# Two alternating places for the first expert matrices, and the next pair's ahead of the down matrices

## What is computed

```python
def grouped_moe(x, w_router, w1, w3, w2):        # w1, w3: [16, 1024, 512], w2: [16, 512, 1024]
    aff = jax.nn.sigmoid(t @ w_router)
    ...                                          # best group of 4 experts, best 2 of it, weights sum to 1
    for e in range(N_EXPERTS):
        h = jax.nn.silu(t @ w1[e]) * (t @ w3[e])
        y = y + gates[:, e:e + 1] * (h @ w2[e])
```

## Time and profile before

| | |
|---|---|
| median of the runs | 1598.01 us |
| profiled execution | 1597.01 us |
| its span | 1595.2 us |
| TensorE busy | 1527.3 us, 96% |
| DMA moved | 425.27 MB, mean 267 GB/s |
| TensorE waits for DMA of w1 and w3, layer 0 | 5.1 us |
| the same, layer 1 | 3.9 us |

### The profile page before, as it was taken

One profiled execution on the slowest core, in us unless ns is written; L12 is line 12 of the kernel. 1 busy time (PEld: TensorE's weight loads), 2 busy tenths in 40 slices (PEclk: granted clock), 3 DMA queues, 4 the chain that ended last, 5 costly groups with the idle time before them and its releaser, 6 DMA issues.

```text
span 1595.2 us, 20497 instructions
## 1 busy us (share of the span) xinstructions
PE 1527.3 (96%) x8300; PEld 1038.2 (65%) x8300; DVE 904.8 (57%) x1338; ACT 646.5 (41%) x1028; POOL 40.9 (3%) x67
## 2 busy tenths in 40 slices
PE   8999999997999999999989999999999999999998
PEld 7775334333887743433357775799887777678997
DVE  4886111115887731111189864687787974757555
ACT  5352111112643421111067764544456766444443
POOL 0100000000000000000040000000002000000000
PEclk9999999999999999999999999999999999999999
DMA  9967999999564599999954545567864354447541
GB/s 313 328 229 314 421 427 428 428 423 288 176 205 154 213 397 422 428 426 428 411 186 159 190 153 195 178 237 287 300 255 170 129 203 170 173 159 279 196 159 27
DMA packets 116140, 425.27 MB, mean 267 GB/s; under 512 B 5117, under 2 KB 7641, under 8 KB 102601
## 3 DMA queue, kind: packets, MB, share of 16 engines
q1 hardware_dynamic: 112384, 416.76, 68.6%
q0 software_dynamic: 2304, 6.95, 1.5%
q10 hardware_dynamic: 1352, 0.18, 0.1%
HBM read 421.78 MB, written 1.05 MB: 265 GB/s over the span
## 4 chain that ended last, share of the span: by engine, by line
PE 69%; DMA 14%; DVE 8%; ACT 4%; DVEq 3%; issue 2%; SPq 0%; ACTq 0%
PE bank L656 42%; DMA ring<-in_moe_w 9%; PE bank L1533 9%; PE bank L1551 4%; DMA arena<-in_moe_w 3%; PE bank L2832 2%; DVE ring_r L3086 1%; PE bank L1563 1%; PE bank L1503 1%; PE bank L858 1%; DMA ring<-in_w_ff 1%; PE bank L2834 1%; PE bank L2735 1%; ACT in_whi L2916 1%; PE bank L2755 1%
## 5 line engine op out<-in xcount | busy, mean ns | idle before, releaser
L1533 PE MATMUL bank<-ring,arena 128*64 128x512 f32 x896 | 226.0, 595 | 9.0 <-DMA ring<-in_moe_w 9.0
L656 PE MATMUL bank<-ring_r,x_hi 128*128 128x512 f32 x528 | 207.7, 393 | 0.0
L607 DVE TENSOR_TENSOR parts_dit<-ring,parts_dit 128x2048 fp32r<-128x2048 f32 x66 | 151.3, 2292 | 74.7 <-ACT parts_dit L604 74.7
L604 ACT CAST parts_dit<-ring 128x2048 fp32r<-128x2048 f32 x66 | 125.1, 1899 | 95.4 <-PE bank L656 83.0
L656 PE MATMUL bank<-parts_dit,f_hi 128*128 128x512 f32 x512 | 160.4, 394 | 0.3 <-DVE parts_dit L607 0.3
L656 PE MATMUL bank<-x_hi,parts_dit 128*128 128x256 f32 x896 | 160.6, 281 | 0.0
L1533 PEld LDWEIGHTS bank<-ring,arena 128*64 128x64 f32 x896 | 74.2, 137 | 117.4 <-issue 117.1
L1856 DVE TENSOR_TENSOR arena<-arena,bank 128x512 f32<-128x512 f32 x16 | 17.2, 1075 | 225.5 <-PE bank L1533 225.5
L656 PEld LDWEIGHTS bank<-x_hi,parts_dit 128*128 128x128 f32 x896 | 137.8, 188 | 0.5
L656 PE MATMUL bank<-in_whi,x_hi 128*128 128x512 f32 x304 | 124.5, 410 | 1.3 <-DVE x_lo L2534 0.8
L656 PE MATMUL bank<-x_lo,parts_dit 128*128 128x256 f32 x448 | 125.3, 280 | 0.0
(11 more groups left out here) (383 smaller groups left out, 2663.8 us busy)
## 6 DMA issues: line engine op xcount, KB each, us to landing
ring<-in_moe_w SPq DMA_DIRECT2D x52, 2048.0 KB, 17.8
arena<-in_moe_w SPq DMA_DIRECT2D x36, 2048.0 KB, 18.5
ring<-in_w_ff SPq DMA_DIRECT2D x32, 2048.0 KB, 9.0
ring<-in_w_ada SPq DMA_DIRECT2D x24, 2048.0 KB, 8.9
ring<-in_w_in SPq DMA_DIRECT2D x20, 2048.0 KB, 9.2
ring<-in_mlstm_w_in SPq DMA_DIRECT2D x8, 2048.0 KB, 15.6
ring<-in_gla_w_in SPq DMA_DIRECT2D x5, 2048.0 KB, 13.2
ring<-in_moe_w SPq DMA_DIRECT2D x8, 1024.0 KB, 17.6
```

The costliest lines, as they stand in the source:

```text
L604: return nc.scalar.copy(part_view(where, 0, h, form), half_of(ring[:, SLOT_OF[n], :], form, h))
L607: return nc.vector.tensor_tensor(part_view(where, 1, h, form), half_of(ring[:, SLOT_OF[n], :], form, h), part_view(where, 0, h, form).bitc ...
L656: last = pe.matmul(out, a[ka], b[kb], start=(first and i == 0), stop=(final and i == 2))
L1533: last = pe.matmul(bank[halves[h], :], s_x[p // 2 % 2][:, c, at:at + CAP], w[h][:, c, :], start=(c == 0), stop=(c == DC - 1))
```

## The change

There are now two places for w1 of odd pairs, `SECOND` and `SECOND + 1` (`DOUBLE = 2`), so that both roles 0 and 1 alternate. There are eight places in all. The arena grows by 16 KB per partition (21536 to 25632 elements). `SECOND` lies in the new part, where no mixer writes. The fourth extra place lies over the row vectors and 4 KB ahead of them.

- `second_of_odd`: the first w1 matrix of pair 1 is issued right behind the last matrix of the mixer's output projection, before the stage of the experts.
- The second w1 matrix of pair 1 goes last of the first burst, when the output projection is done and 3 (layer 0) or 8 (layer 1) uses of row vectors are counted.
- From pair 1 on SyncE's order is w3 of p, w1 of p + 1, w2 of p. The last pair has w3 and w2 alone.
- The row vectors 3 and 8, and with them those behind them, wait on GpSimd until the w1 matrices of the layer's last pair are used.
- The mask `dil` is no longer in the table; it is loaded into `SECOND` behind the second input matrix of the second block, when the experts are done with it.

The core of the diff:

```diff
-        rows = sb("rows", [P, ROW_SLOTS, D])
-        kst = sb("kst", [P, CONST_N])
+        kst = sb("kst", [P, KEPT_N])
...
+        ROWS_AT, SECOND_AT = 72.125, 84.125
+        rows = area(ROWS_AT, ROW_SLOTS * D, (ROW_SLOTS, D))
+        dil = area(SECOND_AT, TT * 2 * T, (TT, 2 * T))
...
-        more_slots = area(36, (ROLES + 1 - SLOTS) * SLOT, (ROLES + 1 - SLOTS, SLOT))
+        more_slots = [area(at, SLOT) for at in (36, 52, SECOND_AT, ROWS_AT - 4)]
...
-            return SECOND if k == 0 and p % 2 else k
+            return SECOND + k if k < DOUBLE and p % 2 else k
...
-            return NP * l + (p - 1 if k == 0 else p)
+            return NP * l + (p - 1 if k < DOUBLE else p)
...
+        ROWS_LEFT = (3, 8)
+
+        def second_of_odd(sp, l):
+
+            if l:
+                sp.wait_ge(e_free[0], NP * l)
+            sp.dma_start(e_slot(SECOND, FE), A["moe_w1"][l, 2].rearrange("(p c) n -> p c n", p=P)).then_inc(
+                e_landed[SECOND], 16)
...
+            def first_of_pair(sp, l, k, p):
+                sp.wait_ge(e_free[k], last_use(k, l, p))
+                sp.dma_start(e_slot(place_of(k, p), FE), A["moe_w1"][l, 2 * p + k].rearrange("(p c) n -> p c n", p=P)).then_inc(
+                    e_landed[place_of(k, p)], 16)
+
             for p in range(NP):
-                for k in by_release if p == 0 else range(ROLES):
+                order = range(ROLES) if p < 2 else range(DOUBLE, ROLES)
+                for k in by_release if p == 0 else order:
                     if p == 1 and k == 0:
+                        continue
+                    elif p == 1 and k == 1:
                         sp.wait_ge(in_used, QUARTERS * (STREAM[("gla_out", "ml_out")[l], N_OUT - 1] + 1))
+                        sp.wait_ge(row_used, ROWS_LEFT[l])
                     elif p:
+                        if k == SLOTS and p < NP - 1:
+                            for j in range(DOUBLE):
+                                first_of_pair(sp, l, j, p + 1)
                         sp.wait_ge(e_free[k], last_use(k, l, p))
...
+                if l == 0 and j == 1:
+                    sp.wait_ge(e_free[0], NP * DEPTH)
+                    sp.dma_start(view(dil, "p t n -> p (t n)"), const[:, KEPT_N:]).then_inc(const_landed, 16)
...
-            mask = view(k("dil"), "p (t n) -> p t n", t=TT)
+            mask = dil
+            dve.wait_ge(const_landed, 48)
...
+                if r in ROWS_LEFT:
+                    pool.wait_ge(e_free[1], NP * (ROWS_LEFT.index(r) + 1))
```

More of the change, by code:

```diff
@@ L68 @@
 CONST, CONST_N = layout([
-    ("ident", P), ("cols", 8), ("keep", P), ("reset", T), ("diag", 32), ("addmask", P), ("dil", TT * 2 * T), ("cos_seq", TT * HD), ("sin_seq", TT * HD),
+    ("ident", P), ("cols", 8), ("keep", P), ("reset", T), ("diag", 32), ("addmask", P), ("cos_seq", TT * HD), ("sin_seq", TT * HD),
     ("cos_ax", TT * HD), ("sin_ax", TT * HD), ("pick", MH * P), ("before", PER * PER),
-    ("earlier", P), ("slots", CAP), ("sum4", NE)])
+    ("earlier", P), ("slots", CAP), ("sum4", NE), ("dil", TT * 2 * T)])
 ONE, LNEPS, RMSEPS, PART = 0, 1, 2, 3
@@ L74 @@
 SECOND_N = FIRST_N + P + T + 32
+KEPT_N = CONST["dil"][0]
 def constant_table():
@@ L274, in build @@
         tmp_g = sb("tmp_g", [P, 4, 32])
-        ARENA = 21536
+        ARENA = 25632
         arena_at = nc.sbuf_base
@@ L319, in build @@
         SECOND = ROLES
+        DOUBLE = 2
         def by_rows(w, n0, n):
@@ L366, in freed, with send_named @@
             eng.wait_ge(w_free[SLOT_OF[n]], FREED[n])
-        def send_named(sp, name, src):
+        def send_named(sp, name, src, between=None):
             send(sp, NUMBER[name], src, src.shape[2])
+            if between is not None:
+                between()
             if name in PAIR:
@@ L381, in gla_sync @@
                     sp.wait_ge(const_landed, 16)
-                    sp.dma_start(kst[:, SECOND_N:], const[:, SECOND_N:]).then_inc(const_landed, 16)
+                    sp.dma_start(kst[:, SECOND_N:], const[:, SECOND_N:KEPT_N]).then_inc(const_landed, 16)
             for j in range(N_OUT):
-                send_named(sp, ("gla_out", j), by_rows(A["gla_w_out"][0], PSB * j, PSB))
-        e_landed = [sem(f"e_landed{k}") for k in range(ROLES + 1)]
+                send_named(sp, ("gla_out", j), by_rows(A["gla_w_out"][0], PSB * j, PSB),
+                           (lambda: second_of_odd(sp, 0)) if j == N_OUT - 1 else None)
+        x_landed = [sem(f"x_landed{tt}") for tt in range(TT)]
+        e_landed = [sem(f"e_landed{k}") for k in range(ROLES + 1)] + [x_landed[0]]
         e_free = [sem(f"e_free{k}") for k in range(ROLES)]
         e_up_rest = sem("e_up_rest")
-        more_slots = area(36, (ROLES + 1 - SLOTS) * SLOT, (ROLES + 1 - SLOTS, SLOT))
+        more_slots = [area(at, SLOT) for at in (36, 52, SECOND_AT, ROWS_AT - 4)]
         def place_of(k, p):
-            return SECOND if k == 0 and p % 2 else k
+            return SECOND + k if k < DOUBLE and p % 2 else k
         def arrivals(k, l, p):
-            if k:
+            if k >= DOUBLE:
                 return NP * l + p + 1
@@ L401, in last_use @@
         def last_use(k, l, p):
-            return NP * l + (p - 1 if k == 0 else p)
+            return NP * l + (p - 1 if k < DOUBLE else p)
         def e_slot(k, width):
-            flat = ring[:, k, :] if k < SLOTS else more_slots[:, k - SLOTS, :]
+            flat = ring[:, k, :] if k < SLOTS else more_slots[k - SLOTS]
             return flat.rearrange("p (c n) -> p c n", n=width)
@@ L418, in e_arrived @@
         def e_arrived(eng, k, count):
-            eng.wait_ge(e_landed[k], 16 * (count + (1 if k == 0 else 0)))
+            eng.wait_ge(e_landed[k], 16 * (count + (1 if k in (0, SECOND + 1) else 0)))
+        ROWS_LEFT = (3, 8)
[4 more added lines that the diff above has]
+                e_landed[SECOND], 16)
         def moe_sync(sp, l):
@@ L455, in mlstm_sync @@
             for j in range(N_OUT):
-                send_named(sp, ("ml_out", j), by_rows(A["mlstm_w_out"][0], PSB * j, PSB))
+                send_named(sp, ("ml_out", j), by_rows(A["mlstm_w_out"][0], PSB * j, PSB),
+                           (lambda: second_of_odd(sp, 1)) if j == N_OUT - 1 else None)
         def dit_sync(sp, l):
@@ L510, in build @@
         turn_src, xt_turned, xt_copied = sem("turn_src"), sem("xt_turned"), sem("xt_copied")
-        x_landed = [sem(f"x_landed{tt}") for tt in range(TT)]
         SRC_AT = {2: 0, 3: 4, 5: 6, 6: 10, 8: 12, 9: 14, 11: 16}
@@ L1472, in four @@
                     at = place_of(half, j // 2)
-                    e_arrived(pe, at, count if half else i + arrivals(0, l, j // 2))
+                    e_arrived(pe, at, i + arrivals(half, l, j // 2))
                     up(pe, half, 0, at=at)
```

## The result

The changed kernel took 1624.91 us (median of 4 runs, 1623.32 to 1626.97), the kernel before 1597.18 us beside it. The ratio is 1.0175, 95% interval 1.0161 to 1.0190. The profiled execution took 1625.39 us (span 1623.6), against 1597.01 (1595.2).

What follows compares the result with a forecast made beforehand. Each expert stretch was taken to end 42.3 us after w2 of pair 6 lands. Per layer 9.8 - 2.0 + 1.0 and 9.8 - 1.8 + 1.0, together 17.8 on 1597.0, gave 1615 us; range 1604 to 1622.

Steps and rivals of the forecast that it cites:

- Part 1: Expert weight queue: w2 of pair 6 stands two transfers later, costing 9.8 us of landing per layer.
- every down matmul group waits for w2: Expected sign in the experts: each down group waits for w2, while w3 matmuls never wait for DMA.
- Part 2: Start of experts: one more matrix held ahead, then a hole in the stream; gains 2.0 us (layer 0), 1.8 (layer 1).
- second small gain in layer 1: Layer 1 stream: an earlier small hole goes as two w1 are queued ahead of w2; 1.8 us more.
- Part 3: Pair 1: TensorE stands for w2 5.0 us in layer 0, 4.9 in layer 1; not added to the sum.
- Part 4: End of experts: later row vectors and mask, and less constant traffic at 60 us, cost 0.
- Part 5: Pauses at pairs 1 and 6 slow TensorE's clock; 1.0 us per layer taken, bounds 0 and 3.8.
- D: Rival, 15%: the clock takes its full price at pairs 1 and 6; 23.4 us more, 1620 us.
- A: Rival, 12%: the stream gets the whole slot ahead, 4.9 us in both layers, no clock loss; 1607 us.
- B: Rival, 7%: faster; late w2 does not hold TensorE and matrices sent ahead remove waits, at most 10.6 us; 1586 us.
- C: Rival, 6%: the queue's new order has no effect, or both parts cancel; 1597 to 1600 us.

Runs made afterwards that it cites:

- e1: Changed kernel with its new places, row vectors and mask, but every pair sent in the old order w1, w3, w2; 1598.98 us, ratio 1.0011.
- e2: Changed kernel, but in pair 6 alone w2 is sent ahead of w1 of pair 7, as before the change; 1616.13 us, ratio 1.0117.
- e5: Changed kernel plus filler matmuls before down matmuls: 5 in pair 1, 2 in pair 6, 0 in pair 7, 1 in others; 1614.98 us, ratio 1.0104.
- e9: Changed kernel plus 5 filler matmuls before the down matmuls of pair 1 and none elsewhere; 1621.89 us, ratio 1.0159.
- e6: Changed kernel's places with old order w1, w3, w2, except first w1 of pair 2 goes ahead of pair 1's w3; 1590.35 us, ratio 0.9961.
- e3: Changed kernel, but only one w1 matrix of the next pair is sent ahead of w2, the other behind it; 1608.20 us, ratio 1.0064.

## Why the prediction was right and wrong

The direction, the place and the mechanism were right, the size was not: 17.8 us were forecast and 27.7 measured (medians), outside the range.

**Part 1, w2 two transfers later: right.** The up groups wait for no DMA, and e1 takes the loss away by the order alone. The sign "every down matmul group waits for w2" was not met: down 0, 2 and 7 do not. Down 0 and down 7 are not behind a late w2; down 2 follows the slow down 1, and TensorE is then itself later than w2. That TensorE cannot make the lateness up in one pair is what e2 shows: with w2 of pair 6 back in its old place down 6 came 195.2 us behind the first matmul in layer 0, where it was 187.0 before and 197.2 after.

**Part 2, the lead and the hole: right in size.** The first w3 of pair 1 was issued at 166.37 and landed 7.9 us later, 21.8 us behind the first matmul. Before, it was 165.14 + 10.0, 23.9 behind: 2.1 us gained where 2.0 were forecast. Parts 1 and 2 give 7.8 and 8.0 us for down 6; e5, with the clock held nearly everywhere, shows 8.3 (7.4 without the late filler) and 8.8. Of the second small gain in layer 1, taken at 1.5 us of its 1.8, about half shows (without it 9.5 us would have been due in layer 1, and e5 has 8.8). The landings of the changed kernel issued at 166.37 and at 226.97:

```profile
ring<-in_moe_w SPq DMA_DIRECT2D x1, 2048.0 KB, 7.9
...
ring<-in_moe_w SPq DMA_DIRECT2D x1, 2048.0 KB, 7.8
```

**Part 3, the stall at pair 1: right.** The row of 177.25 lands at 199.28. From the end of the transposes TensorE stood for 6.1 us in layer 0 and 6.3 in layer 1. Less the usual hand-over of 0.68 that is 5.4 and 5.6, where 5.0 and 4.9 were forecast.

**Part 4: right** within the 0.2 to 3.4 us that e1 leaves. The three row vectors of layer 0 took 12.4 to 16.6 us, not 7.4, and landed by 388.5, still 6 us ahead of the end of the experts. What lies outside the experts is the 1.4 us of the table; it is not explained further.

**Part 5, the clock: the step that failed.** Of the 17.8 us forecast, 15.8 were for the other parts and 2.0 for the clock (1.0 per layer, 3.8 as the bound). Measured, each against its own kernel before, are 17.4 us in e5, where fillers hold the clock nearly everywhere, and 27.7 in the changed kernel. So the clock cost about 10.3 us, some 5 per layer, where 2.0 were taken; the other parts were 1.6 us short. In the stages 9.5 of the 10.3 show: against e5 the tails are 2.5 and 2.8 us longer, and down 6 comes 1.9 and 2.3 us later.

There were two errors. At pair 6 I let 3.4 us of the half clock fall on work, 1.7 us of loss at most, and took less; down 6 takes 9.99 us, 2.9 more than 7.09, so about 5.8 us of it were at half clock. At pair 1 I let the loss be eaten by TensorE's room, with a hole of at most 2.1 us. But w3's places are then released late: the w3 of pair 3 was issued at 226.97 and landed 7.8 us later, which is the time of a transfer on an empty queue, and the DMA share is 0.68 there. It landed 5.9 us behind the w2 before it (228.9) where a step is 4.89, so that hole alone is 1.0 us. Further falls followed waits of 2.5 us at pair 3 of layer 0 and of 2.0 at pair 4 of layer 1, and down 6 is 10.2 and 11.1 us late where e5 has 8.3 and 8.8. The lateness in the stream, 1.9 and 2.3 us, is about the bound of 2.1; the 1.0 that I took for the whole clock did not even cover it. That a slow down group delays the release of w3's places, and so the stream, is read from these rows; how much of it is pair 1's is not settled (e9).

The pauses of the earlier trace rows had shown that 2.7 us can be enough. I priced two pauses per layer from them and left the others out. Not every such pause counts, as 2.60 and 2.69 us were followed by groups of 7.09 in the same execution; what decides it stays open.

**The rivals.** D had this mechanism but was bounded at 1620, as it priced 3.8 us per layer where about 5 were measured. A, B and C are out: down 6 is later and not sooner, and a lead of 4.9 us needs the hole filled, as e6 does.

The Trainium skill, TensorE: Matmul & The Clock Gate, "HAM oscillation", says that DMA waits between groups of matmuls bring the half clock. The trace agrees for down 6 (9.99 us behind a wait of 3.3 us) and not for every wait (7.09 us behind one of 2.69).

## What to carry to other kernels

In a stream that is always full, a new order only moves one landing against another: count for each consumer how many transfers stand ahead of it, and follow the consumer's program order, not the stage's logic. An extra place is worth its full step only if the queue has something to send into the hole that it opens, here a matrix whose place was released 7 us earlier. Price every new pause of TensorE with its clock, and follow the late work back into the releases that the stream waits for.

## What the runs showed of the hardware

- Waits of 2.0 to 2.5 us for DMA between groups of matmuls were often followed by slow ones (e3: 8.78 us for a group of 7.09), but not always: 2.60 and 2.69 us in the changed kernel and 3.20 in e9 were followed by 7.09. So the length of the wait alone does not say whether the clock falls. In e1 it fell with no wait for DMA at all.
- Waits of 6.1 to 6.3 us were followed by groups of 10.0 and 9.6 us (changed kernel), waits of 6.5 by 8.45 and 8.93 (e2).
- The same matmul group ran in 7.09 us at 2.4 GHz; with 4.56 us of fillers in the pause before down 1 it stayed there. Fillers before all down groups gained 9.9 us in the whole kernel from work that is thrown away, though at one pause the clock fell in spite of them (0.53 at 344 to 346 in e5).
- On an empty queue a transfer of 2048 KB took 7.8 to 8.0 us from issue to landing, in the full stream 4.89 us from landing to landing.
